# Mixture-of-experts stage of a hybrid decoder layer: the token gather issued behind the accumulating transfer, with a fifth record slot

## The reference

```python
row_tok = jnp.full((P,), N, dtype=jnp.int32).at[dest].set(s_tok)
x_blocks = x_ext[row_tok].reshape(n_blocks, MOE_BLOCK, D)
def expert_block(args):
    xb, e = args
    h = jax.nn.silu(xb @ w_gate[e]) * (xb @ w_up[e])
    return h @ w_down[e]
y_blocks = lax.map(expert_block, (x_blocks, block_exp))
out = jax.ops.segment_sum(y_sorted.astype(jnp.float32) * s_w[:, None], s_tok, num_segments=N)
```

## Time and profile before

| | us |
|---|---|
| median of 3 runs | 2928.72 (2923.98 to 2938.04) |
| time of the profiled execution | 2923.2 |
| its span, first to last instruction | 2921.6 |
| TensorE busy in the span | 2531.8 (87%) |
| GpSimd busy in the span | 1066.7 (37%) |

### The profile page before, as it was taken

The page is one execution under the profiler, slowest core; times in us unless marked ns, Lnnn a source line. Parts: engine busy times, 40 slices in busy tenths (PEclk is TensorE's granted clock), DMA queues, the critical chain, the costliest instruction groups (busy, mean ns, idle before and its releaser), DMA issues. The chain is left out here.

```text
span 2921.6 us, 37004 instructions
## 1 busy us (share of the span) xinstructions
PE 2531.8 (87%) x12556; PEld 2102.6 (72%) x12557; DVE 1587.9 (54%) x2163; ACT 1194.4 (41%) x1899; POOL 1066.7 (37%) x774
## 2 busy tenths in 40 slices
PE   4999789999998999999969969993998999998960
PEld 3888677777777878777757757873877788787750
DVE  4211166666666666666642249995446445426537
ACT  2211254546464646464520012222547545526532
POOL 1111144545444544454512235663122222222227
PEclk7999899999999999999989989995999999999985
DMA  6655645354536353525255553434558656636725
GB/s 240 249 187 197 195 131 138 105 145 149 140 101 188 106 133 99 151 82 154 72 178 173 162 196 123 137 116 169 184 151 265 181 144 185 187 65 222 223 59 228
DMA packets 300889, 460.91 MB, mean 158 GB/s; under 512 B 20148, under 2 KB 175912, under 8 KB 298728
## 3 DMA queue, kind: packets, MB, share of 16 engines
q1 hardware_dynamic: 278360, 394.98, 42.2%
q0 software_dynamic: 15072, 46.10, 7.2%
q10 hardware_dynamic: 7344, 18.35, 1.6%
HBM read 335.70 MB, written 123.66 MB: 157 GB/s over the span
## 5 line engine op out<-in xcount | busy, mean ns | idle before, releaser
L89 PE MATMUL mx_acc<-u_u,mx_w_hi 128*128 128x512 f32 x1792 | 570.6, 400 | 0.0
L586 POOL TENSOR_TENSOR mx_wt<-mx_wt,mx_rest 128x127 f32<-128x127 f32 (+15 forms) x128 | 271.5, 2121 | 450.1 <-DVE mx_rest L787 450.1
L89 PEld LDWEIGHTS mx_acc<-u_u,mx_w_hi 128*128 128x128 f32 x1792 | 325.8, 190 | 64.0
L795 DVE TENSOR_TENSOR mx_wt_lo<-mx_p_t,mx_wt_hi 128x512 fp32r<-128x512 f32 (+2 forms) x320 | 191.6, 604 | 321.2 <-ACT mx_wt_hi L748 319.2
L787 DVE TENSOR_TENSOR_SCAN mx_rest<-mx_rest,mx_zero 128x128 f32<-128x128 f32 (+15 forms) x128 | 346.6, 2708 | 13.4 <-ACT mx_wt L730 13.4
L89 PE MATMUL mx_acc<-u_u,mx_w_lo 128*128 128x512 f32 x896 | 353.1, 394 | 0.0
L579 POOL TENSOR_TENSOR mx_w_lo<-mx_raw,mx_w_hi 128x1024 fp32r<-128x1024 f32 x112 | 282.7, 2525 | 130.8 <-ACT mx_w_hi L721 130.6
L748 ACT ACTIVATE mx_wt_hi<-mx_p_t 128x512 fp32r<-128x512 f32 (+2 forms) x320 | 170.8, 534 | 356.0 <-PE mx_p_t L640 324.1
L89 PE MATMUL moe_p_gu<-moe_gu_hi,moe_x_hi 128*128 128x512 f32 x656 | 262.8, 401 | 16.4 <-DVE moe_gu_lo L1745 16.4
L89 PE MATMUL moe_p_gu<-moe_gu_hi,moe_x_lo 128*128 128x512 f32 x656 | 258.4, 394 | 0.0
L89 PE MATMUL moe_p_gu<-moe_gu_lo,moe_x_hi 128*128 128x512 f32 x656 | 258.3, 394 | 0.0
(11 more groups left out here) (241 smaller groups left out, 5436.6 us busy)
## 6 DMA issues: line engine op xcount, KB each, us to landing
mx_raw<-in_w_in SPq DMA_DIRECT2D x112, 512.0 KB, 5.1
moe_gu_raw<-in_w_gate SPq DMA_DIRECT2D x64, 512.0 KB, 5.8
moe_gu_raw<-in_w_up SPq DMA_DIRECT2D x64, 512.0 KB, 6.8
moe_dn_raw<-in_w_down SPq DMA_DIRECT2D x32, 1024.0 KB, 4.9
u_saved<-u_u SPq DMA_DIRECT2D x4, 4096.0 KB, 17.0
u_u<-u_saved SPq DMA_DIRECT2D x4, 4096.0 KB, 18.4
mx_w_mod<-in_w_ada SPq DMA_DIRECT2D x64, 256.0 KB, 4.3
gate_t<-mx_g_out SPq DMA_DIRECT2D x64, 256.0 KB, 2.8
```

The lines of the kernel that those rows point to most:

```text
L89: mm = pe.matmul(out, a, b, start=first and n == 0, stop=last and n == len(pairs) - 1, skip_group_check=True)
L586: pool.tensor_tensor(wt[:, t % 2, 0:w - 1], wt[:, t % 2, 0:w - 1], rest[:, t % 2, 1:w], ALU.mult).then_inc(m["weights_done"], 1)
L795: dve.tensor_tensor(wt_lo[:, first:first + k - j], p_t[:, n % TR, 0:(k - j) * P].rearrange("p (j t) -> p j t", t=P), f32(wt_hi[:, first:fi ...
```

## The change

GpSimd's loop is put in another order and runs one block further ahead. In iteration b it now waits for `evict(b + 2)` first, issues the accumulating transfer of block b, waits for turn b+3, issues the gather of block b+4, waits for the accumulating transfer, frees `y`, waits for the gather, shifts the records (four copies, for five slots) and loads the record of block b+5. The prologue gathers one block more. `evict` waits for the first copy of one shift later than before (four copies a shift). TensorE does one more `turn_x` at the end, so that GpSimd's last wait is met, and the table of block rows is two entries longer.

```diff
-ROWS = BLOCKS + 4
+ROWS = BLOCKS + 6
-        record = s.sb("record", [P, 4, 2], U32)
+        record = s.sb("record", [P, 5, 2], U32)
-                pool.dma_start(record[:, 3], records[bass.ds(row, P), :]).then_inc(m["record_in"], 16)
+                pool.dma_start(record[:, 4], records[bass.ds(row, P), :]).then_inc(m["record_in"], 16)
-                for i in range(3):
+                for i in range(4):
                     pool.tensor_copy(record[:, i], record[:, i + 1]).then_inc(m["record_ready"], 1)
-                    wait_apart(pool, marks["pool"], m["record_ready"], 3 * n + (i + 1))
+                    wait_apart(pool, marks["pool"], m["record_ready"], 4 * n + (i + 1))
-                                        in_offset=bass.IndirectOffsetOnAxis(ap=record[:, 3, 0:1], axis=0)
+                                        in_offset=bass.IndirectOffsetOnAxis(ap=record[:, 4, 0:1], axis=0)
-            for n in (1, 2):
+            for n in (1, 2, 3):
                 load_record(n)
                 wait_apart(pool, marks["pool"], m["x_turned"], n)
                 gather_x(n)
                 wait_apart(pool, marks["pool"], m["x_in"], 16 * n + 16)
-                wait_apart(pool, marks["pool"], m["y_out"], 2 * n)
+                if n > 1:
+                    wait_apart(pool, marks["pool"], m["y_out"], 2 * n - 2)
                 shift_records(n)
-            load_record(3)
+            load_record(4)
             with pool.Fori(0, total) as b:
-                wait_apart(pool, marks["pool"], m["x_turned"], b + 3)
-                gather_x(b + 3)
                 wait_apart(pool, marks["pool"], m["y_out"], b * 2 + 6)
                 pool.indirect_dma_start(out=acc, out_offset=bass.IndirectOffsetOnAxis(ap=record[:, 0, 0:1], axis=0), in_=y[:],
                                         in_offset=None, compute_op=ALU.add).then_inc(m["y_added"], 16)
-                wait_apart(pool, marks["pool"], m["x_in"], b * 16 + 64)
+                wait_apart(pool, marks["pool"], m["x_turned"], b + 4)
+                gather_x(b + 4)
                 wait_apart(pool, marks["pool"], m["y_added"], b * 16 + 16)
                 pool.sem_inc(m["y_free"], 1)
-                shift_records(b + 3)
-                load_record(b + 4)
+                wait_apart(pool, marks["pool"], m["x_in"], b * 16 + 80)
+                shift_records(b + 4)
+                load_record(b + 5)
             turn_x(total + 1)
+            turn_x(total + 2)
-                dve.wait_ge(m["record_ready"], 3 * b + 1)
+                dve.wait_ge(m["record_ready"], 4 * b + 5)
```

## The result

The changed kernel takes 2907.5 us (median of 6 runs, 2904.4 to 2909.8) against 2931.6 us of the kernel before beside it: a ratio of 0.9911, 95% interval 0.9899 to 0.9923. The ratio makes it 26 us less, the two medians 24 us. The forecast was 2900 us, a ratio of 0.9903. The profiled execution took 2908.1 us, with a span of 2904.7.

What follows compares the result with a forecast made beforehand. TensorE, busy 87% of the span, was taken as the bound. From the profiled 2923.2 us, 31.5 off in the loop and 3 added at the end gave 2894.7; the same 28.5 gain from the median 2928.7 gave 2900, range 2887 to 2916.

Steps and rivals of the forecast that it cites:

- The 12 waits for the gather go: Expert loop, TensorE: all 12 waits for `x_raw` vanish, 24.6 us of idle, 26.6 us with restarts.
- the three half clocks behind them: Expert loop, TensorE: the 1.2 GHz spells after the three longest gather waits vanish, 3 x 1.65 = 4.9 us.
- Where the gain comes from: Expert loop, GpSimd: the gather moves ahead of the accumulating transfer's landing, copies and record load, with 16.7 us of room.
- The gather in the queue behind the scatter: GpSimd's software queue: the gather starts behind the scatter and overlaps it, landing within 9.4 us, inside 16.7 of room.
- full series: Upper bound for scatter and gather without overlap: 6.9 + 4.4 less 1.9, 9.4 us to landing.
- The slow copies: GpSimd's fourth copy takes 0.35 us in a quiet block, up to 1.36 beside VectorE's weights; 0 on the path.
- The end of the stage: Turn 41 to next stage: 38.2 us becomes 40.8, or 43 if the unneeded gather lands 2 us late.
- `evict` in quiet blocks still at about 8 us: VectorE, a sign: eviction starts about 8 us after the turn; its wait for the gather costs 0 before 16.9.
- GpSimd's loop: GpSimd's iteration in the expert loop takes 12.4 us with a landing of 4.4, far under TensorE's 17.7.
- point of decision: Mean gather landing over 41 blocks from which GpSimd's iteration sets the time: 9.7 us, or 8.2 with slow copies.
- The rival: GpSimd's iteration becomes the bound: 18.9 us and a kernel of 2949 at landings of 9.4 throughout; chance 0.04.
- Sum: Whole kernel: 2923.2 - 31.5 + 3 + 0 = 2894.7 us for the profiled execution, a gain of 28.5 us.

Runs made afterwards that it cites:

- one-pad run: The changed kernel with one memset of 1.8 us added to each GpSimd iteration, between the copies and the record's load: 2936.7 us, ratio to before 1.0013.
- slot alone: The changed kernel with its five slots and gather of block b+4, but the gather put ahead of the scatter again: 2915.6 us, ratio to before 0.9933.

## Where the prediction held and where it failed

*The 12 waits for the gather go, 26.6 us, and the three half clocks behind them, 4.9 us.* Held. The term was 31.5 us and the loop gave 31.0. In the changed kernel's list no gather is late, and the intervals that are longer than 17.7 us are the first and the three with a wait for weights, as before.

*Where the gain comes from.* Held, and tested on both sides. The text put it in the gather moving ahead of landing, copies and load; that needs the record a block earlier. The slot without the order has 26.4 of the 31.0 us, the order without the slot loses 151 us. The rest, 4.6 us by one profile of the changed kernel and 2.3 by the other, goes with the scatter's place ahead of the loading of weights, which the prediction didn't have. The trace shows that cost in TensorE's waits for `y`; its size is not clear of the spread between profiles.

*The gather in the queue behind the scatter.* The bounds held, and the sum with them. Issued 0.3 us behind it, a gather's copies start 6.15 us later (2390.90 to 2397.05), where the nearest case before was 4.2 to 4.4 and full series was put at 9.4. The Trainium skill's rule of descriptors that start in order, though pipelined ("DMA: Bandwidth & Descriptors", Two DMAs through the same engine are not ordered) fits this 1.8 us: more than nothing, much less than the whole scatter. No run separates the order in the queue from two transfers sharing the same DMA engines.

*The slow copies.* The prediction puts those of 0.45 and 1.19 us beside L1745. That group of instructions ended at 2386.4; at 2397.48 to 2399.28 VectorE was at the down weights, the same subtraction of two SBUF tiles:

```profile
2393.93 5.31 DVE L1752 TENSOR_TENSOR moe_dn_lo<-moe_dn_raw,moe_dn_hi 128x1024 fp32r<-128x1024 f32 x4 [0.56 <-ACT moe_dn_hi L1700]
```

Beside the gate and up weights copies are slow too: in the changed kernel the four from 2429.97 on, beside L1747 at 2428.18, take 0.61, 0.97, 0.97 and 0.97 us. A fourth slow copy costs 0.97 us and 0.17 of idle, a little under the 1.36 put down.

*The end of the stage, 2.7 to 5 us, 3 taken.* Mis-sized: 6.5 us (44.7 against 38.2), 6.1 in the second profile. Of GpSimd after turn 41, at 2785.39:

```profile
2803.84 1.00 POOL L1583 DMA_INDIRECT moe_x_raw<-u_rows,moe_record  x1 [4.56 <-DMA acc<-moe_y,moe_record]
...
2814.03 1.65 POOL L1609 DMA_INDIRECT acc<-moe_y,moe_record  x1 [2.67 <-issue]
2815.98 1.00 POOL L1583 DMA_INDIRECT moe_x_raw<-u_rows,moe_record  x1 [0.31 <-issue]
2822.28 0.18 POOL L1579 COPY moe_record<-moe_record 128x2 uint32<-128x2 uint32 x1 [5.30 <-DMA moe_x_raw<-u_rows,moe_record]
```

The chain is the one that the prediction laid out. Its gather stood at 16.1 us after turn 41 and came at 18.5: the last 24 products took 7.2 us at a mean clock of 0.76, where they had taken 5.6 at full clock before, 1.6 us that the prediction had no reason to expect. Another 0.8 us passed between the end of turn 42 (2802.98) and the gather, where the prediction had about nothing. (The row names the scatter's landing as what ended this wait; in the program GpSimd waits there for turn 42.) The last scatter stood at 26.4 and came at 28.6. The useless gather behind it, put down as "2 us late" in the upper bound, was just that: the copies start 8.3 us after the scatter's issue instead of 6.4. The clock's part was in both profiles of the changed kernel, and why it fell in them and not in the kernel before wasn't tried.

*`evict` in quiet blocks still at about 8 us.* Held: 2414.07 is 8.2 us after its turn, after 0.24 us of waiting for the copy. But the step that this coupling costs nothing until landings of 15 us was true only for a GpSimd that arrives in time.

*GpSimd's loop.* This is the step that failed, without harm to the forecast. It was put at 12.4 us, "far under 17.7", with the point of decision at landings of 9.7 us, and the room of a gather at 16.7 us. The one-pad run shows 1.4 us of room on the mean. A quiet iteration already takes 14.15 us. Three terms were short: the gather behind the scatter (6.2, and 9.0 beside the weights with the pad, not 4.4), the load of the record (5.07 to 6.14 us of idle after it beside the weights in the rows shown, not 2.7), and the mean, which counts over stretches in which changes of expert follow each other (18.8 us over seven iterations) and not over all blocks. Room of a transfer and room of the loop that issues it are different things: a gather with 15 us to spare sat in a loop with 1.4. The rival got a chance of 0.04; 1.8 us more an iteration would have taken the whole gain, so that the forecast came out owes something to luck.

*Sum.* 2894.7 for the profiled execution against 2908.1: 3.5 us from the end of the stage, 0.5 from the loop, 7.6 from ahead of turn 0, and 1.8 from what lies around the span. The first two belong to the change, and the third does not. The last may: in twelve runs of the changed kernel the time is 2.2 to 3.7 us over the span, in 33 runs of the kernel before 1.5 to 1.9, and why stays open. By the medians the gain of 28.5 us was 24 to 26.

## What to carry to other kernels

When an engine that serves a loop is late, ask how many blocks of lead its step has before asking for a better order in it: here one more slot was worth 26 us and the order without it cost 151. Then add up the serving engine's whole iteration beside the heaviest traffic, not each transfer's slack, since 1.8 us more in each iteration cost the changed kernel its whole gain. A loop that runs further ahead also runs further past the end; cutting those last iterations gave 14.7 us at the end of the stage, more than half of what the change itself gave.

## What the runs showed of the hardware

An accumulating transfer of 128 rows of 4 KB that went out some 6 us later, into the loading of weights, took 11 us from its issue to the next step (slot alone), against 6.4 to 6.9 in quiet blocks of the kernel before, though the gather stands 0.3 us ahead of it in both. Beside the weights even the load of a 1 KB record held GpSimd for 5.07 to 6.14 us after its issue, against 2.7 in quiet blocks. TensorE's clock fell to 1.2 GHz for the first 3.4 us of the last products of the changed kernel, after a wait of 2.4 us for `y`; the kernel before had the same wait of 2.4 us and kept 2.4 GHz through them.
